# Five weight stripes of the second block's attention turned by DMA instead of TensorE, with three small moves of due slots

## The reference, cut to what matters

```python
q_b = jnp.einsum('bsr,rn->bsn', rms_norm_2(c_q, q_lat_g), w_uq).reshape(b_sz, s_len, H_B, D_HQK)
kv_b = jnp.einsum('bsr,rn->bsn', rms_norm_2(c_kv, kv_lat_g), w_ukv).reshape(b_sz, s_len, H_B, D_NOPE + D_VB)
...
q_b = rms_norm_2(q_b, q_norm_g)
k_b = rms_norm_2(k_b, k_norm_g)
...
o_b = causal_attention(q_b, k_b, v_b).reshape(b_sz, s_len, D_B)
```

## Time and profile before

| | us |
|---|---|
| median of 3 runs | 2116.48 (2116.01 to 2116.72) |
| the profiled execution, its own time | 2117.14 |
| its span | 2115.3 |
| TensorE busy | 2104.2 |
| DVE busy | 1418.4 |
| ACT busy | 1108.4 |

### The profile page before, as it was taken

The page is one execution under the profiler, slowest core; times in us unless marked ns, Lnnn a source line. Parts: engine busy times, 40 slices in busy tenths (PEclk is TensorE's granted clock), DMA queues, the critical chain, the costliest instruction groups (busy, mean ns, idle before and its releaser), DMA issues.

```text
span 2115.3 us, 26982 instructions
## 1 busy us (share of the span) xinstructions
PE 2104.2 (99%) x9556; PEld 1742.9 (82%) x9556; DVE 1418.4 (67%) x1945; ACT 1108.4 (52%) x1527; POOL 60.7 (3%) x70
## 2 busy tenths in 40 slices
PE   9999999999999999999999999999999999999999
PEld 7888887888888888888888888888888888888887
DVE  5999868665565655656777546666445866776763
ACT  6566767454444444444565545554444665565452
POOL 0011100000000000000000000000000000000000
PEclk9999999999999999999999999999999999999999
DMA  8576565776666666666566765556666775657985
GB/s 320 182 233 199 183 235 161 219 213 200 226 216 189 218 199 206 215 196 212 156 218 204 250 196 186 187 179 215 204 201 208 207 224 156 196 179 212 332 263 162
DMA packets 207477, 442.05 MB, mean 209 GB/s; under 512 B 102632, under 2 KB 103024, under 8 KB 207088
## 3 DMA queue, kind: packets, MB, share of 16 engines
q1 hardware_dynamic: 205312, 433.89, 65.5%
q0 software_dynamic: 1744, 6.29, 0.9%
q10 hardware_dynamic: 288, 0.14, 0.0%
HBM read 407.21 MB, written 10.49 MB: 197 GB/s over the span
## 4 chain that ended last, share of the span: by engine, by line
PE 97%; DVE 2%; issue 1%; ACT 0%; DMA 0%; POOL 0%; ACTq 0%; DVEq 0%
PE g L652 31%; PE g L654 31%; PE g L653 31%; PE s L631 1%; DVE arena L1560 1%; PE s L820 0%; PE s L819 0%; DVE wlo L1489 0%; DVE ta_lo L1667 0%; PE s L683 0%; PE s L698 0%; PE s L727 0%; PE s L827 0%; PE s L835 0%; PE s L836 0%
## 5 line engine op out<-in xcount | busy, mean ns | idle before, releaser
L1489 DVE TENSOR_TENSOR wlo<-raw,whi 128x1024 fp32r<-128x1024 f32 x732 | 887.8, 1221 | 521.2 <-ACT whi L909 519.5
L909 ACT ACTIVATE whi<-raw 128x1024 fp32r<-128x1024 f32 x732 | 768.5, 1057 | 685.9 <-PE g L654 616.9
L652 PE MATMUL g<-whi,ta_hi 128*128 128x512 f32 x1920 | 757.3, 394 | 4.1 <-DVE ta_lo L1667 1.3
L654 PE MATMUL g<-whi,ta_lo 128*128 128x512 f32 x1920 | 748.5, 390 | 0.0
L653 PE MATMUL g<-wlo,ta_hi 128*128 128x512 f32 x1920 | 747.9, 390 | 0.0
L652 PEld LDWEIGHTS g<-whi,ta_hi 128*128 128x128 f32 x1920 | 360.9, 188 | 81.1 <-issue 5.9
L654 PEld LDWEIGHTS g<-whi,ta_lo 128*128 128x128 f32 x1920 | 360.7, 188 | 76.3
L653 PEld LDWEIGHTS g<-wlo,ta_hi 128*128 128x128 f32 x1920 | 361.2, 188 | 72.4
L652 PE MATMUL g<-whi,tb_hi 128*128 128x512 f32 x1008 | 395.5, 392 | 0.0
L654 PE MATMUL g<-whi,tb_lo 128*128 128x512 f32 x1008 | 392.5, 389 | 0.0
L653 PE MATMUL g<-wlo,tb_hi 128*128 128x512 f32 x1008 | 392.3, 389 | 0.0
(11 more groups left out here) (242 smaller groups left out, 970.1 us busy)
## 6 DMA issues: line engine op xcount, KB each, us to landing
raw<-in_w_in SPq DMA_DIRECT2D x318, 512.0 KB, 4.2
raw<-in_w_up SPq DMA_DIRECT2D x128, 512.0 KB, 4.2
raw<-in_w_down SPq DMA_DIRECT2D x128, 512.0 KB, 4.1
raw<-in_w_out SPq DMA_DIRECT2D x64, 512.0 KB, 4.3
raw<-in_w_a SPq DMA_DIRECT2D x32, 512.0 KB, 4.3
raw<-in_w_b SPq DMA_DIRECT2D x32, 512.0 KB, 6.3
raw<-in_w_ukv SPq DMA_DIRECT2D x16, 512.0 KB, 3.8
raw<-in_w_uq SPq DMA_DIRECT2D x12, 512.0 KB, 3.8
```

Of the source, the lines that this page charges most:

```text
L652: e.matmul(o, xh, wh, start=first, stop=False)
L654: ins = e.matmul(o, xl, wh, start=False, stop=last)
L909: e.activation(whi[u % RING][:, 0:n], raw[u % RAW][:, 0:n], ACT.Copy).then_inc(s_hi, 1)
L1489: e.tensor_tensor(l, r, h.bitcast(F32), ALU.subtract).then_inc(s_lo, 1)
```

## The change

Five more jobs are put in the table: `uk 0` and `qr 1`, `uq 2`, `uq 3`, `uk 2`. Their ten turns leave TensorE, and ACT's ten copies from PSUM become ten of the joining kind. DVE cuts them. The four transfers of every `qr`, `uq` and `uk` job, of the old ones too, get slots of their own, two apart, so that a weight load stands between them. `uk 0` and `uk 2` start their transfers at `E + 7` and are joined at `E + 16`; `uk 1` and `uk 3` start at `E + 10` and not at `E + 12`. `LN` is one slot later, its groups are spread by one more slot, the statistics are read from the copy in SBUF and the bank is free after ACT's copy. `yt` transfers are due one slot earlier.

```diff
+        CBM["uk", 0] = (ar(17408, 1024), flat[1], None)
         CBM["uk", 1] = (ar(16384, 1024), flat[3], None)
         ao_job(0)
         ao_job(1)
+        CBM["qr", 1] = (ar(17408, 1024), flat[2], None)
+        for n in range(2):
+            CBM["uq", 2 + n] = (ar(16384 + 1024 * n, 1024), ar(11264 + 1024 * n, 1024), None)
+        CBM["uk", 2] = (ar(16384, 1024), ar(17408, 1024), None)
...
-        LN = E("v1") + 2
+        LN = E("v1") + 3
...
-        LNS = [LN, LN, LN + 1, LN + 1, LN + 5, LN + 5, LN + 7, LN + 7]
+        LNS = [LN, LN, LN + 2, LN + 2, LN + 6, LN + 6, LN + 8, LN + 8]
...
-                    b = bank(TBK["ln", g], (ln_b, g + 1))
+                    b = bank(TBK["ln", g], (ln_c, g + 1))
...
-                    turn(b, SG[3], pair).then_inc(qr_t.sem, 1)
...
-                    turn(b, SG[k // 2], k % 2).then_inc(uq_t.sem, 1)
...
-                    turn(b, SG[2], k % 2).then_inc(uk_t.sem, 1)
...
+                yield E("uqr1") + 26
+                q.wait_ge(at_s, 8)
+                join_heads(("qr", 1), qr_c)
...
+                for i in range(2):
+                    yield E(f"uqn1{i}") + (16, 20)[i]
                     q.wait_ge(at_s, 8)
+                    join_heads(("uq", 2 + i), uq_c)
...
-                    for pair in range(2):
-                        yield E(f"ukn{hf}0") + 8 + 2 * pair
-                        q.wait_ge(uk_t, 2 * hf + pair + 1)
-                        q.wait_ge(*((ml_o, 8), (at_s, 8))[hf])
-                        e.activation(HKT[:, 2 * pair:2 * pair + 2, :], two(TBK["uk", 2 * hf + pair]), ACT.Copy).then_inc(uk_c, 1)
+                    yield E(f"ukn{hf}0") + 16
+                    q.wait_ge(*((ml_o, 8), (at_s, 8))[hf])
+                    join_heads(("uk", 2 * hf), uk_c)
...
-                    e.bn_stats(ln6[t][:, 6 * hf:6 * hf + 6], sps[TBK["ln", g]][:, :]).then_inc(ln_b, 1)
+                    e.bn_stats(ln6[t][:, 6 * hf:6 * hf + 6], LNN[:, t, hf * 512:(hf + 1) * 512]).then_inc(ln_b, 1)
...
+                    if n == 0:
+                        yield E(st.name) + 5
+                        q.wait_ge(uk_m, i + 1)
+                        cut_heads(("uk", i), flat[2])
...
                     elif name == "qr":
-                        yield E("uqr0") + 14
+                        first = E(f"uqr{n}") + 14
+                        yield first
                     elif name == "uq":
-                        yield E(f"uqn{n // 2}{n % 2}") + 5 + n % 2
+                        first = E(f"uqn{n // 2}{n % 2}") + 5
+                        yield first
...
                     elif name == "uk":
-                        yield E(f"ukn{n // 2}1") + 12
+                        first = E(f"ukn{n // 2}{n % 2}") + (7, 10)[n % 2]
+                        yield first
...
-                        yield E(f"yb1{n}") + 3
+                        yield E(f"yb1{n}") + 2
...
                     for h in range(2):
                         for t in range(2):
+                            if name in ("qr", "uq", "uk") and h + t > 0:
+                                yield first + 4 * h + 2 * t
                             e.dma_start_transpose(to[:, h, :, t * P:(t + 1) * P], src[:, h, t]).then_inc(d_turn.sem, 16)
```

More of the change, by code:

```diff
@@ L599, in two_blocks @@
         use += [(LNS[k], "ln", k) for k in range(8)]
-        use += [(E("uqr1") + 16 + 2 * k, "qr", k) for k in range(2)]
-        use += [(E(f"uqn1{k // 2}") + 2 + 2 * (k % 2), "uq", k) for k in range(4)]
-        use += [(E(f"ukn{k // 2}0") + 8 + 2 * (k % 2), "uk", k) for k in range(4)]
         use += [(E(f"ukn{k // 2}1") + 13 + k % 2, "kr", k) for k in range(4)]
@@ L776, in ml_side @@
                             e.matmul(b2[:, 0:258], s[:, 256:384], v[:, 1], start=False, stop=True).then_inc(ml_o, 1)
-            def uqr_side():
-                for pair in range(2):
-                    yield E("uqr1") + 16 + 2 * pair
-                    b = bank(TBK["qr", pair], (qr_c, 3 + pair))
-                    q.wait_ge(qr_v, 2)
-                    turn(b, SG[3], pair).then_inc(qr_t.sem, 1)
[L785 to L789, removed]
-                    turn(b, SG[k // 2], k % 2).then_inc(uq_t.sem, 1)
[L792 to L796, removed]
-                    turn(b, SG[2], k % 2).then_inc(uk_t.sem, 1)
             def kr_side():
@@ L1293, in zb_side @@
                     else:
-                        q.wait_ge(*((w_cut, cut(("uq", 1))) if n == 1 else (uq_t, 4)))
+                        q.wait_ge(w_cut, cut(("uq", n)))
                         q.wait_ge(uq_r, 2 if n == 1 else 4)
@@ L1303, in gb_side @@
                     q.wait_ge(zb_c, 2 * (n // 2) + 2)
+                    if n == 1:
+                        q.wait_ge(uk_c, 2)
                     if n == 3:
@@ L1342, in uq_side @@
                     join_heads(("uq", i), uq_c)
-                for k in range(4):
-                    yield E(f"uqn1{k // 2}") + 2 + 2 * (k % 2)
-                    q.wait_ge(uq_t, k + 1)
+                for i in range(2):
+                    yield E(f"uqn1{i}") + (16, 20)[i]
                     q.wait_ge(at_s, 8)
-                    e.activation(HQT[:, 2 * k:2 * k + 2, :], two(TBK["uq", k]), ACT.Copy).then_inc(uq_c.sem, 1)
+                    join_heads(("uq", 2 + i), uq_c)
             def uqn_side():
@@ L1364, in ukn_side @@
                     q.wait_ge(rs_out, RSI["lat1"])
-                    q.wait_ge(*((qr_v, 1), (qr_c, 2), (qr_v, 2), (ao_l, 4))[i])
+                    q.wait_ge(*((qr_v, 1), (qr_c, 2), (qr_c, 4), (ao_l, 4))[i])
                     copy_scaled(st, SG[UK[i]], RS["lat1"][1]).then_inc(uk_e.sem, 1)
@@ L1399, in uv_side @@
                         q.wait_ge(at_o, 8)
+                        q.wait_ge(uq_c, 8)
                     copy_scaled(st, HV[:, :, 512 * (i % 2):512 * (i % 2) + 512], RS["lat1"][1]).then_inc(uv_e.sem, 1)
@@ L2057, in uqr_side @@
                     ins.then_inc(qr_v, 1)
[L2058 to L2061, removed]
+                    yield E(f"uqr{hf}") + 12
+                    q.wait_ge(qr_v, hf + 1)
+                    if hf == 1:
+                        q.wait_ge(at_o, 8)
+                    cut_heads(("qr", hf), flat[3])
             def cut_heads(job, src):
@@ L2071, in uq_side @@
             def uq_side():
-                for i in range(2):
-                    yield E(f"uqn0{i}") + 3
+                for i in range(4):
+                    yield E(f"uqn{i // 2}{i % 2}") + 3
                     q.wait_ge(uq_r, i + 1)
-                    cut_heads(("uq", i), flat[i])
+                    if i >= 2:
+                        q.wait_ge(at_o, 8)
+                    cut_heads(("uq", i), flat[i % 2])
             def uqn_side():
@@ L2142, in at_side @@
                         q.wait_ge(d_turn, 64 * CBN["uk", 1] + 64)
+                        if i >= 8:
+                            q.wait_ge(uk_c, 6)
                         e.tensor_tensor(pb, sps[0][:, 0:384], CST[:, C_MASK:C_MASK + 384], ALU.add).then_inc(at_m.sem, 1)
@@ L2178, in ao_side @@
                     if n == 1:
-                        q.wait_ge(qr_t, 2)
+                        q.wait_ge(w_cut, cut(("qr", 1)))
                     join_words(("ao", n))
```

10 lines of the change are left out of this document (5 added, 5 removed).

## The result

The changed kernel takes 2143.48 us (median, 2142.21 to 2145.64) against 2116.3 for the kernel before: ratio 1.0127, interval 1.0115 to 1.0139. It is 27 us slower. The forecast was 2122.3 us with a range from 2108.3 to 2128.5, and it gave slower a chance of 0.50: the number has the right sign and the wrong size, and the measured time lies 15 us above the range. The profiled execution took 2142.21 us, with a span of 2140.4 us, 25.1 more than before's.

A forecast was written before the change was run, and what follows sets the result against it. The prediction took TensorE's own stream to bound the kernel. Gains of 7.6 us against waits of 4.2 + 3.4 + 4.2 + 1.6 us gave +5.8 us, a forecast of 2122.3 us, range 2108.3 to 2128.5.

The forecast's parts named there:

- Ten turns: On TensorE: ten turns removed at 0.48 us each, a gain of 4.8 us, called certain for TensorE's own work.
- Last transfers: At the first `out0` units: `yt` transfers leave earlier, so a late weight split's gap goes, -0.77 us (0 to -0.77).
- Layer norm: At the layer norm's turns: later, spread slots remove TensorE's waits for convolution step and statistics, -2.0 us (0 to -2.0).
- the rival's mechanism: At the layer norm: the moved wait reappears at the second turns, 2.0 us come back, 2124.3 us; chance 0.03.
- Head 0's scores: First half: TensorE waits 4.2 us for rotary copies behind ACT's join of `uk 0`; bounds 0.2 to 5.5 us.
- Head 0's output: First half: 1.6 us of waiting plus 1.8 for the mask add's wait on `uk 1`, together 3.4 us (2.4 to 4.3).
- I take that as hidden by the splits made ahead: Before the second half's keys: `qr 1` landing some 4 us late costs nothing; otherwise the wait grows by up to 4.6 us.
- `uk 2` has the same distances: 4.2 us again: Second half: the wait at ACT's join of `uk 2` repeats that of `uk 0`, 4.2 us.
- The 1.6 us for head 8's output: Second half: TensorE waits 1.6 us for head 8's output, with no added wait for `uk 3`.
- The clock: Rival: TensorE's clock falls after 4 us waits, 1.6 us a time, up to four times, 2128.7 us; chance 0.05.
- Waits stay hidden: Rival at ACT's joins of `uk 0` and `uk 2`: no waits, gains stand, 2108.9 us; chance 0.25.
- short: Rival: waits come but last only 1 to 3 us in each half, 2112.9 us (2111 to 2115); chance 0.07.

The follow-up runs named there:

- e7: Kernel before with only the layer norm's turns and the last transfers moved, all ten stripes on TensorE; 2115.22 us, ratio 0.9991.
- e2: Changed kernel with `uk 0` and `uk 2` back on TensorE, `qr 1`, `uq 2`, `uq 3` still on the crossbar; 2125.36 us, ratio 1.0039.
- e8: Changed kernel with `uk 0`, `uk 2` on TensorE, `uk 1`, `uk 3` as in the kernel before, the three query jobs on the crossbar joined late; 2118.07 us, ratio 1.0003.
- e9: Kernel of e8 with `uq 3`'s transfers begun four events later, nothing else; 2113.07 us, ratio 0.9983 to the kernel before.
- e4: Changed kernel with the second half's second rotary turn in PSUM bank 2 instead of bank 3; 2138.9 us, ratio 1.0102.
- e12: Kernel of e10 with `uk 0` and `uk 2` in one burst each, joined at the changed kernel's event, 16; 2117.61 us, ratio 0.9999.
- e10: Changed kernel, all five jobs on the crossbar, with later joins, later `uq 3` transfers, `uk 1` and `uk 3` in bursts, another rotary bank; 2123.97 us, ratio 1.0034.

## Why the prediction was right in sign and wrong in size

- **Ten turns**, -4.8: right, 0.46 to 0.50 each. **Last transfers**, -0.77: -0.75. **Layer norm**, -2.0: -1.6; 0.32 us of waiting came back at the second turns, the rival's mechanism in small. e7 confirms both parts alone.
- **Head 0's scores**, 4.2: right in mechanism, too small in size: 6.1, above the forecast's own upper bound of 5.5. (It called 4.2 the middle of 0.2 to 5.5, which is 2.9.) DVE's lag and the start of the fourth transfer came as derived. It landed at 1735.0, 4.85 us after its start, and not at 1734; the median of 4.3 us in the earlier trace rows would already have given 1734.7. So the copies were ready at 1740.75 (0.75 late), and TensorE, with the layer norm's gain carried along, was due at 1734.65, not 1735.8 (1.15). I had left the gains of the early parts out of the due time; only the two turns were taken off. TensorE carried them, while DVE, which paced the transfers, did not.
- **Head 0's output**, 3.4: 1.9 of waiting, a step of 2.4, the lower bound of the forecast. The mask add did wait for `uk 1`, 2.2 us of DVE's idle time, and came 6.8 us after the rotary copies (4.4 + 1.8 forecast); but TensorE, at first on half clock, asked for the output 13.1 us after the scores and not 11.2.
- **"I take that as hidden by the splits made ahead"**, the joins of the query jobs: this step failed, a term put at nothing. In the changed kernel it cost 3.5 us of waiting and 1.6 of clock; e2, with only these jobs, lost 9 us to them. The forecast had named the price and a bound of 4.6 for it, and then took the low end without naming a row that covers it. It had also looked at ACT alone. e8 and e9 show SP's part: SP waits in order before a job until the last has landed, and the weight loads queue behind. Late joins brought the 8.9 us down to 6.3, SP's later start brought them to 1.0.
- **"`uk 2` has the same distances: 4.2 us again"**: this step failed too, by the largest amount, 11.0 and 2.0 of clock in place of 4.2. The distances were the same, the bank was not. e4 shows 4.9 us at the scores with the bank changed, near what the forecast's mechanism gives; the shared bank made the rest. The 1.6 us for head 8's output did not come. In the changed kernel the wait stood 8.3 us ahead of head 8's scores, time in which ACT and DVE went on; in e4, where the scores themselves waited, TensorE came to the output 13.8 us after them and not 11.2, again at first on half clock.
- **A wait for weights**, 1.9 us at 1888.92, stands in no term. It comes (1.5 to 1.9 us) in all seven traces with all five jobs on the crossbar, and in none with only the three query jobs or only `uk 0` and `uk 2`. What makes it was not followed up.
- **The clock**, given 5 in 100 and 1.6 us a time: the price was near (1.6 to 2.0), the chance was not. It fell three times, 5.6 us in all. Once waits of 4 us were forecast, were the only rows that showed TensorE's clock after a wait, and they showed it low. That belonged in the sum.
- **Waits stay hidden** (0.25), **short** (0.07): both ruled out by the 9.4 us in which ACT stood twice before a join.
- **The range.** Its ends don't follow from its own words: the clean case is 2116.5 - 7.6 = 2108.9, stated as 2108.3, and 2127.9 with half of the clock's 6.4 is 2131.1, stated as 2128.5. The measured time lies outside either way.
- The forecast rested on the crossbar losing only where something waits for the landing. That holds, with a wider sense of waiting: also the work behind the join in ACT's order and behind the transfer in SP's.

The sum with what was measured: -7.2 + 6.1 + 1.9 + 3.5 + 1.9 + 11.0 + 5.6 = 22.8 of the 25.1 us of span. The rest lies in steps under 1 us and isn't explained. That the sign came out right rests on a sum of which two terms and the clock were missing or far too small.

**Left open.** e12's executions spread over 5 us, and its profiled one is its slowest, so the waits read there may be at the long end. No run took the query jobs' joins and SP's wait apart in the changed kernel itself; the split of the 9 us between them comes from e2, e8 and e9, one after the other, and could come out otherwise if SP's wait were mended first. The 8 us that e12 still loses against the gains are not explained.

## What to carry to other kernels

When work goes from the busiest engine to a transfer, its price isn't its duration but what stands behind it in two queues: behind the instruction that waits for the landing, and behind the next issue that waits for it. Write down, for both engines, the next five instructions and who needs them, and put the waiting one where the transfer has landed: e8 to e9 was one number and 5 us. A PSUM bank shared by two steps is one more such queue, and gains of earlier parts make every later deadline earlier.

## What the runs showed of the hardware

**The clock after waits.** In the thirteen traces of the changed kernel and the experiments TensorE stood still 14 times for 3.0 to 11.0 us in the attention; 13 times the matmuls behind it ran at 1.2 GHz for a while (0.43 us from start to start in place of 0.23). The exception is the 3.0 us of e10 shown above. Of 15 waits of 2.0 to 3.0 us, 9 were followed by it (2.24 us in e12) and 6 not (2.96 us in e2). The length of the wait alone didn't decide. The forecast had thought of waits of 4 us only.

**Weights beside transfers.** Beside the crossbar transfers a weight load took 5.4 us to its landing instead of 4.4, and TensorE didn't notice it in e9. A later landing of every load was free there, and so were 6.5 us without an issue in the kernel before (1829.51 to 1835.99); the 9.1 us of e8 were not.
